# Attention probabilities turned by products with a diagonal of reciprocal denominators, in place of plain turns and a later division

## The chip, the cores and the metric

The kernel runs on one core of one Trainium2 chip. The metric is the device time of one execution in microseconds (us), as a median of several runs. Beside it one execution was recorded by the hardware profiler; its trace supplies every duration below. The engines are TensorE (PE for its products, PEld for the loads of their stationary side), VectorE (DVE), ScalarE (ACT), GpSimd (POOL) and SyncE (SP, which here only issues transfers). All data of the part in question is float32.

## The reference, cut to what matters

Two layers work on 1024 latent tokens and 256 context tokens. Inside a layer, one group of heads does windowed attention: a block of 128 queries sees its own block, the two neighbours and all 256 context keys, with one extra logit for each head (the sink) that takes part in the denominator only.

```
s_loc = jnp.einsum('bnikgd,bnjkd->bnkgij', qb, kw).astype(jnp.float32) * scale
s_ctx = jnp.einsum('bnikgd,bckd->bnkgic', qb, kc).astype(jnp.float32) * scale
...
probs = jax.nn.softmax(jnp.concatenate([s_loc, s_ctx, sink_l], axis=-1), axis=-1)
o = (jnp.einsum('bnkgij,bnjkd->bnikgd', probs[..., :n_loc].astype(v.dtype), vw)
     + jnp.einsum('bnkgic,bckd->bnikgd', probs[..., n_loc:n_loc + n_ctx].astype(vc.dtype), vc))
```

The result goes, with three other groups of heads, through an output projection, a residual with two layer norms, and a router for the experts that come next. In the first layer the context tokens go through the same steps, but read only context.

## The kernel before

`attend` does this part, once for each layer. It walks over tiles of 128 tokens: N = 10 tiles in the first layer (eight latent, two context), N = 8 in the second. Each engine has its own program, written out in order by a loop over `t` from 0 to N + 1, and the engines meet only at semaphores. The loop is staggered: in pass `t` the attention of tile `t`, the output projection and first norm of tile `t - 1`, and the second norm and router of tile `t - 2` are under way. There is no scheduler: an instruction that waits holds up everything behind it on its engine.

Four heads are handled as two pairs, 0 and 1. For a pair, TensorE computes scores, VectorE masks them and takes maxima (`maxima`), and ScalarE takes exponentials (`exps`), which also leave row sums in `sums`; the exponential of the sink is in `se`. `expd` counts the pairs for which this is done. TensorE then turns the unnormalised probabilities (`turn_probs`, 10 blocks of 128x128 in a latent tile, 4 in a context tile) through the two PSUM buffers `T`, four, four and two blocks at a time; ScalarE copies each group to `pT` (`copy_turned`) and counts `T_read`, and TensorE may not reuse a buffer of `T` before. `values` multiplies by V and leaves the head outputs in `O[:, 0:2]`.

Normalisation comes last. Once for each tile, VectorE adds up the four denominators and takes reciprocals (`denominators`), GpSimd multiplies the identity with them (`diagonals`, into `dg`, 128x512), TensorE spreads them over partitions with four products against ones (`spread_den`, into `O[:, 2:4]`), ScalarE copies these to `rb`, and VectorE multiplies `O[:, 0:2]` by `rb` (`heads`), which counts `o_ready`.

On VectorE the second norm of tile `t - 2` (`norm2`, which ends in a `tensor_scalar` at L214) stands after `maxima(t, 0)`. Its end, `norm2_done`, starts `modulate_rows` on GpSimd: two operations over 128x1024, L1137 and L1139, each with both inputs in SBUF. In the last two tiles of a layer VectorE does these itself. GpSimd's `add_one(0)` (L1131) waits for a transfer and stands at the head of GpSimd's program, ahead of the diagonals of tile 0.

Of the kernel before, what the change touches and what calls it, by code (L numbers as in the profile page):

```python
# [10 lines left out]
ALU = mybir.AluOpType  # L11
# [3 lines left out]
P = 128  # L15
# [7 lines left out]
HD = 64  # L23
# [127 lines left out]
def across(ap, n):  # L151

    return ap.unsqueeze(1).to_broadcast([ap.shape[0], n] + list(ap.shape[1:]))
# [880 lines left out]
def attend(nc, g, m, l):  # L1034
# [7 lines left out]
    with ExitStack() as ctx:  # L1042
# [12 lines left out]
        mx, mx2, den = sb("max_near", [P, 2]), sb("max_far", [P, 2]), sb("denominator", [P, NH])  # L1055
        dg, rb = sb("den_diag", [P, NH, P]), sb("den_rows", [P, 2, P])
        ys = [sb(f"mixT{i}", [P, 4, P]) for i in range(2)]
# [9 lines left out]
            sem(n) for n in ("sink_in", "small_in", "g1_in", "vec_in", "w_in", "ln1_in", "router_in"))  # L1067
        far_scored, scored, maxed, expd, den_ready, diag_ready = (
            sem(n) for n in ("far_scored", "scored", "maxed", "expd", "den_ready", "diag_ready"))
        T_full, T_read = [sem(f"turn_full{i}") for i in range(2)], [sem(f"turn_read{i}") for i in range(2)]  # L1070
        gate_full, sgu_done, rb_full, rb_read, pv_done, o_ready = (
            sem(n) for n in ("gate_full", "sgu_done", "rb_full", "rb_read", "pv_done", "o_ready"))
        y0_full, y1_full, y_used = (sem(n) for n in ("y0_full", "y1_full", "y_used"))
# [22 lines left out]
        with nc.Block() as block:  # L1096
# [31 lines left out]
            def _(pool):  # L1128
# [14 lines left out]

                def diagonals(t):
                    pool.wait_ge(den_ready, t + 1)
                    if t:
                        pool.wait_ge(rb_full, t)
                    nc.gpsimd.tensor_tensor(dg[:, :, :], across(g.k[:, K_ID:K_ID + P], NH), over(den[:, :], P), ALU.mult).then_inc(diag_ready, 1)

                def gain_rows(u):  # L1150
# [9 lines left out]
                for t in range(N + 2):  # L1160
                    if rtr(t):
                        norm_power(nc, pool, g, n2, t - 2)
                        if t - 2 < N - 2:
                            modulate_rows(t - 2)
                    if att(t):
                        diagonals(t)
                    if t == N - 1 and N > LT:
                        add_one(1)
                    if prj(t):
                        if t == 1:  # L1170
                            pool.wait_ge(ln1_in, 32)
                        norm_power(nc, pool, g, n1, t - 1)
                        if t - 1 < N - 1:
                            gain_rows(t - 1)

            @block.vector
            def _(v):
# [34 lines left out]

                def denominators(t):
                    v.wait_ge(expd, t * 2 + 2)
                    if t:
                        v.wait_ge(diag_ready, t)
                    small(nc.vector.tensor_tensor(den[:, :], sums[:, 1, :], se[:, :], ALU.add))
                    done()
                    small(nc.vector.tensor_tensor(den[:, :], den[:, :], sums[:, 0, :], ALU.add))
                    done()  # L1220
                    nc.vector.reciprocal(den[:, :], den[:, :]).then_inc(den_ready, 1)

                def heads(t):
                    v.wait_ge(rb_read, t + 1)
                    nc.vector.tensor_tensor(ys[t % 2][:, 0:2, :], O[:, 0:2, :], rb[:, :, :], ALU.mult).then_inc(o_ready, 1)

# [58 lines left out]
                for t in range(N + 2):  # L1285
                    if att(t):
                        maxima(t, 0)
                    if rtr(t):
                        norm2(t - 2)
                    if prj(t):  # L1290
                        residual(t - 1, 0)
                    if att(t):
                        maxima(t, 1)
                        if t == 0:
                            v.wait_ge(small_in, 80)
                        gate_out(t)
                        denominators(t)
                    if prj(t):
                        residual(t - 1, 1)
                        norm1(t - 1)  # L1300
                    if t == N - 1:
                        heads(t)
                    if rtr(t) and t != N:
                        h2_turned(t - 2)
                    if t < N - 1:
                        heads(t)

            @block.scalar
            def _(act):
                def exps(t, pair):  # L1310
                    act.wait_ge(maxed, t * 4 + pair * 2 + 2)
                    if t:
                        b, n = turn_of["probs", t - 1, pair, len(blocks(t - 1)) - 1]
                        act.wait_ge(T_full[b], n + 1)
                        if pair == 0:
                            act.wait_ge(den_ready, t)
# [26 lines left out]
                for t in range(N + 2):  # L1343
                    if t >= 3:
                        logits(t - 3)
                    if att(t):
# [3 lines left out]
                        act.wait_ge(pv_done, t * 2 + 2)  # L1350
                        nc.scalar.activation(rb[:, :, :], O[:, 2:4, :], ACT.Copy).then_inc(rb_read, 1)
                    if t >= N:
# [14 lines left out]
            def _(pe):  # L1367
# [30 lines left out]
                def turn_probs(t, pair):  # L1398
                    pe.wait_ge(expd, t * 2 + pair + 1)
                    flat = pr[pair][:, :, :].rearrange("p a n -> p (a n)")  # L1400
                    for j, group in enumerate(blocks(t)):
                        turn(("probs", t, pair, j), [flat[:, b * P:(b + 1) * P] for b in group])

# [14 lines left out]
                def gate(t):  # L1418
# [4 lines left out]
                    mm.then_inc(gate_full, 1)  # L1423

                def spread_den(t):
                    pe.wait_ge(diag_ready, t + 1)
                    for pair in range(2):
                        for kv in range(NKV):
                            mm = nc.tensor.matmul(O[kv * HD:(kv + 1) * HD, 2 + pair, :], g.k[:, K_ONE:K_ONE + HD], dg[:, 2 * kv + pair, :], start=True, stop=True)
                    mm.then_inc(rb_full, 1)  # L1430

# [39 lines left out]
                for t in range(N + 2):  # L1471
# [24 lines left out]
                    if att(t):  # L1496
                        spread_den(t)
                        values(t, 1)
# [757 lines left out]
```

## Time and profile before

| what | value |
|---|---|
| median of 3 runs | 2593.94 us (2593.25 to 2599.5) |
| the profiled execution | 2593.13 us, span 2591.3 us |
| TensorE busy over the span | 2337.7 us (90%) |
| VectorE, ScalarE, GpSimd busy | 939.7, 406.8, 464.0 us |
| `attend`, first layer | some 351.8 to 640 us from the span's start |
| `attend`, second layer | some 1600 to 1842 us |
| L1395, turns of probabilities | 336 rows, 54.6 us busy |
| L1148, diagonals on GpSimd | 18 operations of 1.04 us |

Outside `attend` nothing is touched by the change: most of the span lies in the experts (L2046 and the lines behind it). A reader takes from the table that the execution that was profiled is as long as the others, and that TensorE is the engine with least slack over the whole; whether it is so in `attend` is read from the trace of that stretch.

### The profile page before, as it was taken

How to read it: one execution, taken by the hardware profiler on the slowest of the kernel's cores; microseconds unless marked ns; L12 is line 12 of the kernel's file. 1: busy time of each engine (PE TensorE's matmuls, PEld its weight loads, DVE VectorE, ACT ScalarE, POOL GpSimd, SP SyncE). 2: the span in 40 equal slices, each digit the busy share in tenths (PEclk: the TensorE clock that was granted, in tenths of full speed). 3: DMA queues.
4: the chain of work that ended last, by engine and by line, in shares of the span. 5: the costliest groups of instructions: out<-in, count | busy, mean ns of one | idle time of the engine just before them, and what ended most of it. 6: DMA issues, size and time to landing. Idle time of an engine off the chain costs nothing. (4 is left out here: it accounts for less than half of the span.)

```text
span 2591.3 us, 39013 instructions
## 1 busy us (share of the span) xinstructions
PE 2337.7 (90%) x15084; PEld 1629.2 (63%) x15084; DVE 939.7 (36%) x2319; ACT 406.8 (16%) x1057; POOL 464.0 (18%) x608
## 2 busy tenths in 40 slices
PE   7999879997499999999949997999389999999996
PEld 5999745654466666666639984555266666666652
DVE  1777746665401110110126565565611111111114
ACT  1011133321011111111111113233000000000000
POOL 0000103444011111111111111344111111111111
PEclk9999989998699999999979998999689999999998
DMA  9655430001679999999832103000289999999955
GB/s 357 202 172 157 147 114 17 17 26 49 235 299 393 387 395 388 387 392 401 344 138 96 49 19 146 29 25 17 106 345 398 384 382 391 391 386 394 377 230 213
DMA packets 130991, 608.69 MB, mean 235 GB/s; under 512 B 20840, under 2 KB 23912, under 8 KB 112208
## 3 DMA queue, kind: packets, MB, share of 16 engines
q1 hardware_dynamic: 113456, 569.60, 56.9%
q0 software_dynamic: 16864, 37.78, 3.8%
q8 instruction: 63, 1.03, 0.2%
q14 instruction: 32, 0.26, 0.0%
q10 hardware_dynamic: 576, 0.02, 0.0%
HBM read 599.39 MB, written 42.02 MB: 248 GB/s over the span
## 5 line engine op out<-in xcount | busy, mean ns | idle before, releaser
L2046 PEld LDWEIGHTS gate_up<-room,w_gate_up 128*128 128x128 f32 x4608 | 521.1, 193 | 31.6 <-issue 31.6
L2046 PE MATMUL gate_up<-room,w_gate_up 128*128 128x128 f32 x4608 | 528.0, 277 | 3.2 <-DVE room L1926 3.2
L2055 PE MATMUL down<-w_down,room 128*128 128x512 f32 x576 | 256.8, 599 | 0.0
L2063 PE MATMUL gate_up_short<-w_gate_up,room 128*64 128x512 f32 x1152 | 255.1, 595 | 0.0
L1935 DVE TENSOR_TENSOR room<-room,gate_up 128x128 f32<-128x128 f32 x144 | 41.4, 288 | 539.0 <-ACT room L1966 539.0
L2063 PEld LDWEIGHTS gate_up_short<-w_gate_up,room 128*64 128x64 f32 x1152 | 79.5, 137 | 171.3 <-issue 171.3
L2055 PEld LDWEIGHTS down<-w_down,room 128*128 128x128 f32 x576 | 106.5, 190 | 123.0 <-issue 120.5
L1657 POOL COPY rows_idx<-slot_token 128x1 int32 (+1 forms) x78 | 14.3, 183 | 777.7 <-PE rows_turned L2033 721.1
L1943 DVE TENSOR_TENSOR room<-room,gate_up_short 128x256 f32<-128x256 f32 x36 | 15.2, 421 | 369.1 <-ACT room L1973 369.1
L2076 PE MATMUL down<-w_down,room 128*64 128x512 f32 x576 | 131.5, 598 | 11.9 <-ACT room L1975 11.9
L1443 PE MATMUL proj<-w_out,mixT 128*128 128x512 f32 x288 | 129.5, 592 | 0.0
L1966 ACT ACTIVATE room<-gate_up 128x128 f32<-128x128 f32 x144 | 39.9, 277 | 552.6 <-PE gate_up L2046 552.6
L2033 PE MATMUL rows_turned<-consts,rows 128*128 128x128 f32 (+1 forms) x592 | 90.7, 286 | 27.2 <-DMA rows<-h_rows,rows_idx 27.2
L2033 PEld LDWEIGHTS rows_turned<-consts,rows 128*128 128x128 f32 (+1 forms) x592 | 75.1, 196 | 61.0 <-issue 56.6
L1926 DVE COPY room<-rows_turned 128x512 f32<-128x512 f32 (+1 forms) x148 | 76.1, 556 | 70.6 <-PE rows_turned L2033 70.6
L1443 PEld LDWEIGHTS proj<-w_out,mixT 128*128 128x128 f32 x288 | 54.7, 190 | 68.9 <-issue 68.9
L397 DVE SCALAR_TENSOR_TENSOR ada_sum<-ada_w,cond_silu,ada_sum 128x512 f32<-128x512 f32 x140 | 96.2, 745 | 4.8 <-DMA ada_w<-in_w_ada 1.6
L1660 POOL DMA_INDIRECT rows<-h_rows,rows_idx x78 | 78.7, 1010 | 66.5 <-POOL rows_idx L1657 48.7
L2076 PEld LDWEIGHTS down<-w_down,room 128*64 128x64 f32 x576 | 39.4, 136 | 79.2 <-issue 79.2
L1671 POOL DMA_INDIRECT expert_rows<-room,y_idx x36 | 36.7, 1019 | 225.0 <-DVE room L1941 113.4
L1395 PE MATMUL turn<-consts,probs 128*128 128x128 f32 x336 | 54.6, 299 | 22.0 <-ACT sink_exp L1323 12.7
L538 PE MATMUL bankC<-hT,w_in 128*128 128x128 f32 x640 | 74.1, 277 | 0.0
(365 smaller groups left out, 3206.2 us busy)
## 6 DMA issues: line engine op xcount, KB each, us to landing
w_gate_up<-in_w_exp_gate SPq DMA_DIRECT2D x72, 2048.0 KB, 8.5
w_down<-in_w_exp_down SPq DMA_DIRECT2D x72, 2048.0 KB
w_gate_up<-in_w_exp_up SPq DMA_DIRECT2D x72, 2048.0 KB, 13.3
ada_w<-in_w_ada SPq DMA_DIRECT2D x96, 512.0 KB, 4.8
h_rows<-h SPq DMA_DIRECT2D x18, 512.0 KB, 2.6
w_out<-in_w_out SPq DMA_DIRECT2D x2, 4096.0 KB, 13.4
w_in<-in_w_in SPq DMA_DIRECT2D x2, 3072.0 KB, 20.6
xn<-expert_rows SPq DMA_DIRECT2D x10, 512.0 KB, 4.1
```

The source lines that it names most:

```text
L397: op = nc.vector.scalar_tensor_tensor(acc[:, i, :], w_k, by, acc[:, i, :], ALU.mult, ALU.add)
L538: i = nc.tensor.matmul(out, lhsT(k), rhs(k), start=k == 0, stop=k == KT - 1)
L1395: tr = nc.tensor.transpose(T[b][:, i, :], src, ident)
L1443: mm = nc.tensor.matmul(Y[:, half, :], rows, wo[:, k, half * 512:(half + 1) * 512], start=j == 0, stop=j == KT - 1)
L1660: pool.indirect_dma_start(xg[q][rows, :], None, g.h2[:, :], bass.IndirectOffsetOnAxis(ap=idx[q][rows, 0:1], axis=0), bounds_check=NT * P - ...
L1926: c = nc.vector.tensor_copy(xT[q][:, 4 * h:4 * h + 4, :], T[:, 4 * h:4 * h + 4, 0:P if q == 0 else HP])
L1935: nc.vector.tensor_tensor(hid[:, j, :], silu[:, j % 2, :], H[j % 2][:, 1, :], ALU.mult).then_inc(hid_done, 1)
L2033: tr = nc.tensor.transpose(T[:, k, 0:rows], xg[q][0:rows, k::KT], g.k[0:rows, K_ID:K_ID + rows])
L2046: mm = nc.tensor.matmul(H[j % 2][:, o, :], wgu[0][:, o, k, j * P:(j + 1) * P], xT[0][:, k, :], start=k == 0, stop=k == KT - 1)
L2055: mm = nc.tensor.matmul(Y[:, h, :], hid[:, j, :], wd[0][:, j, h * 512:(h + 1) * 512], start=j == 0, stop=j == JT - 1)
L2063: mm = nc.tensor.matmul(Hs[c * HP:(c + 1) * HP, :, :], xT[1][:, k, :], wgu[1][:, :, k, c * 2 * P:(c + 1) * 2 * P], start=k == 0, stop=k == ...
L2076: mm = nc.tensor.matmul(Y[h * HP:(h + 1) * HP, 0, :], hidT_s[:, j % 2, j // 2 * HP:(j // 2 + 1) * HP], wd[1][:, j, h * 512:(h + 1) * 512], ...
```

## The change

Each block of probabilities is now turned by an ordinary product with a 128x128 diagonal of the reciprocals as moving side, so that what reaches `pT` is already normalised. For this the denominators have to be there before the turn. `denominators` runs for each pair, on VectorE, and makes the diagonals there too (128x256 for a pair); `turn_probs` waits for `diag_ready` of its pair where it waited for `expd`. `diagonals` on GpSimd, `spread_den` on TensorE, the copy to `rb` and `heads` are gone; ScalarE copies `O[:, 0:2]` to the mixer's input `ys`.

```
-                def diagonals(t):
-                    pool.wait_ge(den_ready, t + 1)
...
-                    nc.gpsimd.tensor_tensor(dg[:, :, :], across(g.k[:, K_ID:K_ID + P], NH), over(den[:, :], P), ALU.mult).then_inc(diag_ready, 1)
...
-                def denominators(t):
...
+                def denominators(t, pair):
+                    mine = lambda x: x[:, pair:NH:2]
+                    v.wait_ge(expd, t * 2 + pair + 1)
+                    small(nc.vector.tensor_tensor(mine(den), mine(sums[:, 1, :]), mine(se), ALU.add))
                     done()
+                    small(nc.vector.tensor_tensor(mine(den), mine(den), mine(sums[:, 0, :]), ALU.add))
                     done()
+                    small(nc.vector.reciprocal(mine(den), mine(den)))
+                    done()
+                    nc.vector.tensor_tensor(dg[:, pair, :, :], across(g.k[:, K_ID:K_ID + P], 2), over(mine(den), P), ALU.mult).then_inc(diag_ready, 1)
...
-                def heads(t):
-                    v.wait_ge(rb_read, t + 1)
-                    nc.vector.tensor_tensor(ys[t % 2][:, 0:2, :], O[:, 0:2, :], rb[:, :, :], ALU.mult).then_inc(o_ready, 1)
...
                     if rtr(t):
                         norm2(t - 2)
+                    if att(t):
+                        denominators(t, 0)
                     if prj(t):
                         residual(t - 1, 0)
...
                         gate_out(t)
-                        denominators(t)
+                        denominators(t, 1)
...
-                        nc.scalar.activation(rb[:, :, :], O[:, 2:4, :], ACT.Copy).then_inc(rb_read, 1)
+                        nc.scalar.activation(ys[t % 2][:, 0:2, :], O[:, 0:2, :], ACT.Copy).then_inc(o_ready, 1)
...
                 def turn_probs(t, pair):
-                    pe.wait_ge(expd, t * 2 + pair + 1)
+                    pe.wait_ge(diag_ready, t * 2 + pair + 1)
...
-                        turn(("probs", t, pair, j), [flat[:, b * P:(b + 1) * P] for b in group])
+                        b, n = turn_of["probs", t, pair, j]
+                        if n:
+                            pe.wait_ge(T_read[b], n)
+                        for i, k in enumerate(group):
+                            mm = nc.tensor.matmul(T[b][:, i, :], flat[:, k * P:(k + 1) * P], dg[:, pair, k // 5, :], start=True, stop=True)
+                        mm.then_inc(T_full[b], 1)
...
-                def spread_den(t):
-                    pe.wait_ge(diag_ready, t + 1)
-                    for pair in range(2):
-                        for kv in range(NKV):
-                            mm = nc.tensor.matmul(O[kv * HD:(kv + 1) * HD, 2 + pair, :], g.k[:, K_ONE:K_ONE + HD], dg[:, 2 * kv + pair, :], start=True, stop=True)
-                    mm.then_inc(rb_full, 1)
```

VectorE, in the first layer, from the end of the second norm of tile `t - 2` to the residual of tile `t - 1`, before:

```order
L206 MEMSET norm_spare 128x1
L207 BN_AGGR norm_mv<-norm_stats 128x2
L214 TENSOR_SCALAR h_0_0<-x_res,norm_mv,norm_rstd 128x1024
L1237 TENSOR_TENSOR h_1_0<-proj,mod_0 128x512
L1239 SCALAR_TENSOR_TENSOR x_res<-x_res,h_1_0 128x512
```

The same place now:

```order
L214 TENSOR_SCALAR h_0_0<-x_res,norm_mv,norm_rstd 128x1024
L1208 TENSOR_TENSOR denominator<-sums,sink_exp 128x2
L1210 TENSOR_TENSOR denominator<-denominator,sums 128x2
L1212 RECIPROCAL denominator<-denominator 128x2
L1214 TENSOR_TENSOR den_diag<-consts,denominator 128x256
L1226 TENSOR_TENSOR h_1_0<-proj,mod_0 128x512
L1228 SCALAR_TENSOR_TENSOR x_res<-x_res,h_1_0 128x512
```

Four operations now stand directly behind the `tensor_scalar` whose end starts GpSimd on L1137.

TensorE, from the values of pair 0 to the router in the same pass, before:

```order
L1414 MATMUL head_out<-probsT_0,v_tok 64x128 x10
L1395 MATMUL turn_0<-consts,probs_0 128x128 x10
L1395 MATMUL turn_0<-consts,h_0_0 128x128 x8
L1429 MATMUL head_out<-den_diag,consts 64x128 x4
L1414 MATMUL head_out<-probsT_0,v_tok 64x128 x10
L1463 MATMUL turn_0<-h2T,w_router 36x128 x8
```

The same place now:

```order
L1404 MATMUL head_out<-probsT_0,v_tok 64x128 x10
L1391 MATMUL turn_0<-den_diag,probs_0 128x128 x10
L1380 MATMUL turn_0<-consts,h_1_0 128x128 x8
L1404 MATMUL head_out<-probsT_0,v_tok 64x128 x10
L1446 MATMUL turn_0<-h2T,w_router 36x128 x8
```

The four spreading products are gone, and the turn of the probabilities has the diagonal as an input instead of the constants.

## Rows read from the trace of the kernel before

**Rows 1.** Busy times in one pass of the first layer's `attend`.

```profile
core 0: us, PE busy (x) PEld busy (x) DVE busy (x) ACT busy (x) POOL busy (x), PEclk, DMA share, GB/s
510.67:537.25 26.58, 25.82 (x161) 15.79 (x159) 16.41 (x42) 8.53 (x28) 12.29 (x10) 1.00 0.05 21
```

**Rows 2.** Timeline, one pass around pair 0's turn: start, length, engine, instruction.

```profile
464.32 0.21 ACT L1323 ACTIVATE sink_exp<-sink_diff 128x2 f32<-128x2 f32 x1
464.65 0.81 DVE L214 TENSOR_SCALAR h<-x_res,norm_mv,norm_rstd 128x1024 f32<-128x1024 f32 x1 [0.93 <-POOL norm_rstd L197]
465.54 2.37 POOL L1137 TENSOR_TENSOR h<-h,mod 128x1024 f32<-128x1024 f32 x1 [0.93 <-DVE h L214]
466.34 1.04 PE L1395 MATMUL turn<-consts,probs 128*128 128x128 f32 x8
467.37 1.09 DVE L1239 SCALAR_TENSOR_TENSOR x_res<-x_res,h 128x512 f32<-128x512 f32 x1
467.69 0.44 PE L1395 MATMUL turn<-consts,probs 128*128 128x128 f32 x2 [0.31 <-ACT probsT L1336]
467.98 2.68 POOL L1139 TENSOR_TENSOR h<-h,mod 128x1024 f32<-128x1024 f32 x1
468.05 0.59 PE L1378 MATMUL scores<-kT,qT 64*128 64x384 f32 x1
```

**Rows 3.** Instructions by tile (probs, head_out): count, nanoseconds least/median/most, first and last start.

```profile
L1395 PE MATMUL turn<-consts,probs x336: 272/273/477, 359.9 to 1809.1; 128*128 128x128 f32 x168
L1429 PE MATMUL head_out<-den_diag,consts x144: 272/273/473, 376.9 to 1810.9; 128*64 128x128 f32 x144
```

**Rows 4.** The page's groups: 128x128 products that run back to back.

```profile
L2046 PE MATMUL gate_up<-room,w_gate_up 128*128 128x128 f32 x4608 | 528.0, 277 | 3.2 <-DVE room L1926 3.2
```

**Rows 5.** Timeline, TensorE from pair 1's turn to its values, in the same pass layout.

```profile
451.99 1.09 PE L1395 MATMUL turn<-consts,probs 128*128 128x128 f32 x8
453.98 1.07 PE L1395 MATMUL turn<-consts,h 128*128 128x128 f32 x8
454.97 0.66 PE L1429 MATMUL head_out<-den_diag,consts 128*64 128x128 f32 x8
455.46 1.26 PE L1414 MATMUL head_out<-probsT,v_tok 128*64 128x128 f32 x20
```

**Rows 6.** Timeline, tile 0: the small additions of the denominators.

```profile
369.76 0.16 DVE L1217 TENSOR_TENSOR denominator<-sums,sink_exp 128x4 f32<-128x4 f32 x1 [1.51 <-ACT sink_exp L1323]
369.96 0.16 DVE L1219 TENSOR_TENSOR denominator<-denominator,sums 128x4 f32<-128x4 f32 x1
```

**Rows 7.** Timeline, pass 8: a small VectorE operation during a long one of GpSimd.

```profile
563.81 2.35 POOL L1155 TENSOR_TENSOR x_res<-x_res,ln 128x1024 f32<-128x1024 f32 x1
565.69 0.49 DVE L1197 TENSOR_TENSOR max_far<-max_near,max_far 128x2 f32<-128x2 f32 x1
```

**Rows 8.** Timeline, pass 10: VectorE and GpSimd starting almost together.

```profile
617.46 1.31 DVE L1270 SCALAR_TENSOR_TENSOR h<-x_res,norm_mv,mod 128x1024 f32<-128x1024 f32 x1
617.50 0.19 POOL L195 TENSOR_TENSOR norm_rstd<-norm_mv,consts 128x1 f32<-128x1 f32 x1 [1.65 <-DVE norm_mv L207]
```

**Rows 9.** Timeline, the two context tiles: GpSimd's second operation, TensorE's turn.

```profile
571.99 0.60 PE L1395 MATMUL turn<-consts,probs 128*128 128x128 f32 x4
572.34 2.35 POOL L1139 TENSOR_TENSOR h<-h,mod 128x1024 f32<-128x1024 f32 x1
...
596.43 2.36 POOL L1139 TENSOR_TENSOR h<-h,mod 128x1024 f32<-128x1024 f32 x1
...
597.50 0.60 PE L1395 MATMUL turn<-consts,probs 128*128 128x128 f32 x4
```

**Rows 10.** Timeline, tile 0: GpSimd's first long operation, and TensorE behind the diagonal.

```profile
372.93 2.78 POOL L1131 TENSOR_SCALAR mod<-mod 128x1024 f32<-128x1024 f32 x1 [20.66 <-DMA mod<-mods]
376.88 1.12 PE L1429 MATMUL head_out<-den_diag,consts 128*64 128x128 f32 x8 [3.65 <-POOL den_diag L1148]
```

**Rows 11.** Busy times, the stretch right behind that wait.

```profile
376.81:380.21 3.40, 3.33 (x30) 3.00 (x30) 0.00 (x0) 0.03 (x1) 0.02 (x1) 0.50 0.00 0
```

More of the change, by code:

```diff
@@ L1055, in attend @@
         mx, mx2, den = sb("max_near", [P, 2]), sb("max_far", [P, 2]), sb("denominator", [P, NH])
-        dg, rb = sb("den_diag", [P, NH, P]), sb("den_rows", [P, 2, P])
+        dg = sb("den_diag", [P, 2, 2, P])
         ys = [sb(f"mixT{i}", [P, 4, P]) for i in range(2)]
@@ L1067, in attend @@
             sem(n) for n in ("sink_in", "small_in", "g1_in", "vec_in", "w_in", "ln1_in", "router_in"))
-        far_scored, scored, maxed, expd, den_ready, diag_ready = (
-            sem(n) for n in ("far_scored", "scored", "maxed", "expd", "den_ready", "diag_ready"))
+        far_scored, scored, maxed, expd, diag_ready = (
+            sem(n) for n in ("far_scored", "scored", "maxed", "expd", "diag_ready"))
         T_full, T_read = [sem(f"turn_full{i}") for i in range(2)], [sem(f"turn_read{i}") for i in range(2)]
-        gate_full, sgu_done, rb_full, rb_read, pv_done, o_ready = (
-            sem(n) for n in ("gate_full", "sgu_done", "rb_full", "rb_read", "pv_done", "o_ready"))
+        gate_full, sgu_done, pv_done, o_ready = (
+            sem(n) for n in ("gate_full", "sgu_done", "pv_done", "o_ready"))
         y0_full, y1_full, y_used = (sem(n) for n in ("y0_full", "y1_full", "y_used"))
@@ L1142, in modulate_rows @@
                         nc.gpsimd.engine_nop().then_inc(vec_free, 1)
-                def diagonals(t):
-                    pool.wait_ge(den_ready, t + 1)
-                    if t:
-                        pool.wait_ge(rb_full, t)
-                    nc.gpsimd.tensor_tensor(dg[:, :, :], across(g.k[:, K_ID:K_ID + P], NH), over(den[:, :], P), ALU.mult).then_inc(diag_ready, 1)
                 def gain_rows(u):
@@ L1164, in _ @@
                             modulate_rows(t - 2)
-                    if att(t):
-                        diagonals(t)
                     if t == N - 1 and N > LT:
@@ L1211, in gate_out @@
                     nc.vector.tensor_tensor(out, out, m.u[:, :, at_tile(t)], ALU.mult).then_inc(sgu_done, 1)
-                def denominators(t):
[L1214 to L1217, printed above, removed]
+                def denominators(t, pair):
+                    mine = lambda x: x[:, pair:NH:2]
+                    v.wait_ge(expd, t * 2 + pair + 1)
+                    small(nc.vector.tensor_tensor(mine(den), mine(sums[:, 1, :]), mine(se), ALU.add))
                     done()
-                    small(nc.vector.tensor_tensor(den[:, :], den[:, :], sums[:, 0, :], ALU.add))
+                    small(nc.vector.tensor_tensor(mine(den), mine(den), mine(sums[:, 0, :]), ALU.add))
                     done()
-                    nc.vector.reciprocal(den[:, :], den[:, :]).then_inc(den_ready, 1)
-                def heads(t):
-                    v.wait_ge(rb_read, t + 1)
-                    nc.vector.tensor_tensor(ys[t % 2][:, 0:2, :], O[:, 0:2, :], rb[:, :, :], ALU.mult).then_inc(o_ready, 1)
+                    small(nc.vector.reciprocal(mine(den), mine(den)))
+                    done()
+                    nc.vector.tensor_tensor(dg[:, pair, :, :], across(g.k[:, K_ID:K_ID + P], 2), over(mine(den), P), ALU.mult).then_inc(diag_ready, 1)
                 def residual(u, half):
@@ L1300, in _ @@
                         norm1(t - 1)
-                    if t == N - 1:
-                        heads(t)
                     if rtr(t) and t != N:
                         h2_turned(t - 2)
-                    if t < N - 1:
-                        heads(t)
             @block.scalar
@@ L1314, in exps @@
                         act.wait_ge(T_full[b], n + 1)
-                        if pair == 0:
-                            act.wait_ge(den_ready, t)
                     for i in range(2):
@@ L1496, in _ @@
                     if att(t):
-                        spread_den(t)
                         values(t, 1)
```

## The prediction

> **What bounds the kernel now.** I first read the busy times of one pass of `attend` [rows 1]: in a pass of 26.58 us TensorE is busy for 25.82, at the full granted clock; VectorE for 16.4, GpSimd for 12.3, ScalarE for 8.5. So in a steady pass each microsecond that TensorE works more or waits longer is a microsecond of the run. Then I read the timeline of one pass (tile 4 of the first layer) around the place where the turn of pair 0 stands [rows 2]. TensorE reaches this turn at 466.34. The exponentials that it waits for ended at 464.53, so there is a slack of 1.8 us today. Within it VectorE is held until 465.46 by the `tensor_scalar` of the second norm, whose end starts GpSimd's L1137 at 465.54; L1139 follows at 467.98. The same timeline shows L1239 at 1.09 us; its least time is 0.69. It started at 467.37, inside L1137, and ended at 468.46, which is 0.55 us after L1137's end (467.91). L1139 in turn took 2.68 us instead of 2.36 [rows 2, 9]. Both engines read two tensors of SBUF there. A smaller case says it more sharply [rows 7]: an addition over two columns, started at 565.69 inside L1155, took 0.49 us and ended at 566.18, when L1155 ended (566.16); alone it would have been an addition like those of 0.16 us [rows 6]. I read this as: a VectorE operation with two SBUF inputs stands still until the GpSimd operation that runs is over, whatever its own size.
>
> **The change part by part.**
>
> *The turn on TensorE.* The count of instructions matters more than their length. Today 336 blocks are turned by 336 matmul rows, one for each block; the 72 spreading products, which are ordinary float32 products, have 144 rows, two for each [rows 3]. So the turn becomes 20 rows for a pair of a latent tile instead of 10. Rows of 128 columns that run back to back with full weights come at 528.0 us / 4608 = 0.115 us [rows 4], so 20 rows take 2.3 us, and about 0.1 us of handover to the next kind. Today pair 0's block occupies TensorE from 466.34 to 468.05, 1.71 us, because it waits for ScalarE's copy before its last two turns [rows 2]; at the slower rate that copy is done in time, and the wait goes. So pair 0 costs 2.36 - 1.71 = +0.65 us. For pair 1 the stretch to the next turn is 1.99 us (451.99 to 453.98) [rows 5]; ScalarE's copies then end it at about 2.65, +0.65 too. The spreading products leave: from 454.97 to 455.46, 0.49 us [rows 5]. Net +0.8 us of TensorE for a latent tile, bounded by +0.7 and by +1.9 (if neither wait goes). There are 14 steady latent tiles (7 in each layer): +11.2 us.
>
> The Trainium skill, "TensorE: Matmul & The Clock Gate", section Terms, says that the transpose mode of a matmul is four times faster for FP32. The rows here show a factor of two in instructions, 336 for 336 blocks against 144 for 72 products [rows 3]. By the page the products would cost 20 rows more for each pair than I count.
>
> *Pair 0's denominators on VectorE.* They stand directly behind L214. The first addition follows L214 without a wait and ends at about 465.54, when GpSimd starts. The second needs the first and starts 0.20 us after it [rows 6], at about 465.57: 0.03 us after L1137. Who wins is decided by a pair of starts [rows 8]: L1270 on VectorE started at 617.46, 0.04 us before GpSimd's L195, and L195 still took its 0.19 us unhindered. So GpSimd goes first even with VectorE slightly ahead, and here VectorE is behind. The second addition then waits until L1137 ends, 467.91. The reciprocal (one tensor, about 0.2 us) lets L1139 start at 467.98. The diagonal (128x256, two SBUF inputs) meets L1139 and waits until it ends: 467.98 + 2.36, the undisturbed length [rows 9], = 470.34. Behind that end it needs between 0.02 us (the two columns of rows 7) and 0.55 (the 512 of L1239); by size 0.28. TensorE starts some 0.08 us later, at 470.70. Against 466.34 this is a stall of 4.4 us. Behind it in VectorE's queue stands the residual of tile `t - 1`, first half, and then `maxima(t, 1)`; both have their inputs later than the diagonal or shortly behind, since the scores of pair 1 also move by 5 us. Behind the waiting turn on TensorE stands everything else of the pass. So nothing hides it.
>
> This holds for passes in which GpSimd modulates and TensorE turns a latent tile: tiles 2 to 7 in both layers, 12 x 4.36 = 52.3 us. In tile 1 GpSimd has no such work and the slack of 1.8 us covers four operations of about 1 us. In the context tiles L1139 ends at 574.70 and 598.79 and the turns stand at 571.99 and 597.50 [rows 9]: with the same 0.36 behind, stalls of 3.1 and 1.7 us, and 4 rows more, 0.45 us, for pair 0 (for pair 1 these rows and the missing spread cancel): 5.6 us.
>
> *Pair 1's denominators.* They come after `gate_out`, when GpSimd has finished its modulation, and are ready some 2 us before TensorE reaches this turn behind the second half of the projection. Cost nothing; without that cover about 1 us a tile.
>
> *Tile 0.* Today TensorE waits 3.65 us for the diagonal behind L1131 [rows 10]. Pair 1's additions meet L1131 and wait for its end, 375.71; the diagonal is ready at about 376.8, when the spread starts today. Behind it now stands a turn of 2.4 us (twice that at half clock) instead of a spread of 0.5 to 0.9. +2 to +3.5 us, I take 2.5, in two layers 5 us. If L1131 with its one tensor did not hold VectorE, this would be near nothing.
>
> *The clock.* Behind the wait of 3.65 us the granted clock was 0.50 of full, that is 1.2 GHz instead of 2.4, for 3.4 us in which TensorE was busy for 3.33 [rows 10, 11]. Half of that is lost, 1.7 us. The stalls of 4.4 us are longer than that wait, so I give each of the 14 stalls 1.7 us: 23.8 us. The ends are 0 and 3.4 us each.
>
> *What leaves elsewhere.* GpSimd's 18 diagonals, ScalarE's copy (which stays, to another place) and VectorE's `heads` lie beside TensorE's work; they give nothing.
>
> **Sum.** 52.3 + 11.2 + 5.6 + 5 + 23.8 = 97.9 us, on the profiled execution's 2593.1 us: 2691. The median of the runs is 0.8 us above that execution, so I say 2692.
>
> **The rivals.**
>
> *Only the first of GpSimd's operations holds the diagonal.* If the second addition slips in ahead of L1137, the reciprocal follows, and the diagonal goes through in the gap at 467.91, as L1239 does today. The turn starts at 468.27, a stall of 1.9 us: 23.2 us for 12 tiles, 11.2 for the rows, 1.5 for context, 5 for tile 0, and the clock perhaps half the time, 10. Sum 51, 2644 us. For it: the starts are only 0.03 us apart. Against: GpSimd went first from behind [rows 8].
>
> *Nothing is held.* Then the diagonal is ready four operations after L214, 465.46 + 0.2 + 0.2 + 0.2 + 0.4 = 466.5, and the stall is 0.2 us. The sum is 2.6 + 11.2 + 0.9 + 5 = 20, 2613 us. Against it stand the held operations [rows 2, 7].
>
> *Faster: TensorE only loses work.* If a product with the diagonal cost one row as a turn does, the blocks would stay as they are, 18 spreads of 0.49 us go, and with TensorE as the sole bound the waits of tile 0 go too, 3.65 us twice: -16 us, 2577. It decides when a product costs under about 1.2 rows. The counts speak against it [rows 3].
>
> *Dearer products.* Four rows each instead of two add 2.3 us for each of the 28 steady blocks and 0.9 for four of context, 68 us on top of the main case: 2760. The page named above says four times; here the count of rows speaks against it.
>
> **How the numbers follow.** Main case 0.72, first rival 0.12, nothing held 0.07, faster 0.04, dearer 0.03, others 0.02. The likeliest case alone spans 2668 (clock never falls) to 2716 (two such spells behind each stall, less the tiles in which it finds little work). The range must leave out no more than 2 in 10: from 2638, which takes in the first rival, to 2716. 0.3% of this run is 8 us, about what a measurement of this kernel can tell from no change: faster by more than that 0.05, within it 0.03, slower 0.92.
>
> **What would show it.** In the profile after: 672 rows for the turned blocks instead of 336; a pass of 33 to 34 us instead of 26.6; the second addition of pair 0 with a duration of about 2.3 us and the diagonal of pair 0 with about 2.5, both ending with GpSimd's operations; TensorE idle about 4.4 us before the turn of pair 0, released by VectorE's diagonal; the granted clock at half behind many of these. Wrong: short additions and a diagonal of 0.4 us throughout (then nothing is held); a diagonal that ends at L1137's end (then the first rival); a clock that stays full over the stalls (then 2668); 336 rows (then faster).

## The result and the profile after

| | before | after |
|---|---|---|
| median of the runs on the same chip | 2593.94 us | 2696.1 us (2694.34 to 2700.42) |
| ratio, 95% interval | 1 | 1.0389 (1.0376 to 1.0402) |
| profiled execution | 2593.13 us | 2700.42 us, span 2698.6 us |
| first `attend`, first scores to last router products | 288.2 us | 347.3 us |
| second `attend`, the same | 241.9 us | 289.5 us |

The change costs 102 us by the medians; 98 was forecast. The two stretches of `attend` alone grew by 59.1 + 47.6 = 106.7 us, and the span by 107.3 (the profiled execution is the longest of the five), so all but 0.6 us of it lies inside `attend`. Of the seven executions of the kernel before that stand beside e1 to e4 one took 9757.84 us, which no trace explains; it is in none of the ratios.

The page of the kernel after: busy times, and its group for the turn of the probabilities.

```profile
PE 2400.8 (89%) x15276; PEld 1693.3 (63%) x15276; DVE 1007.2 (37%) x2391; ACT 410.1 (15%) x1057; POOL 441.3 (16%) x590
L1391 PE MATMUL turn<-den_diag,probs 128*128 128x128 f32 x672 | 116.5, 345 | 72.7 <-DVE den_diag L1214 72.7
```

There are 672 rows where there were 336 [rows 3], and TensorE stands idle for 72.7 us in front of them, in 18 waits, released each time by VectorE's diagonal. Of these, 50.0 us are the waits of tiles 2 to 7 in the two layers; 15.6 us stand before the first turn of a layer, where the kernel before waits too (6.38 and 6.35 us, for ScalarE's exponentials). The same stretch as in [rows 2], the timeline of a steady pass of the kernel after:

```profile
550.10 0.21 ACT L1308 ACTIVATE sink_exp<-sink_diff 128x2 f32<-128x2 f32 x1
550.43 0.81 DVE L214 TENSOR_SCALAR h<-x_res,norm_mv,norm_rstd 128x1024 f32<-128x1024 f32 x1 [0.94 <-POOL norm_rstd L197]
551.16 0.15 DVE L1208 TENSOR_TENSOR denominator<-sums,sink_exp 128x2 f32<-128x2 f32 x1
551.32 2.34 POOL L1137 TENSOR_TENSOR h<-h,mod 128x1024 f32<-128x1024 f32 x1 [0.93 <-DVE h L214]
551.35 2.33 DVE L1210 TENSOR_TENSOR denominator<-denominator,sums 128x2 f32<-128x2 f32 x1
553.71 0.17 DVE L1212 RECIPROCAL denominator<-denominator 128x2 f32<-128x2 f32 x1
553.74 2.34 POOL L1139 TENSOR_TENSOR h<-h,mod 128x1024 f32<-128x1024 f32 x1
553.91 2.45 DVE L1214 TENSOR_TENSOR den_diag<-consts,denominator 128x256 f32<-128x256 f32 x1
556.29 0.68 DVE L1226 TENSOR_TENSOR h<-proj,mod 128x512 f32<-128x512 f32 x1
556.42 4.63 PE L1391 MATMUL turn<-den_diag,probs 128*128 128x128 f32 x20 [4.13 <-DVE den_diag L1214]
```

Two additions of the same form stand here, 0.19 us apart. One takes 0.15 us; the other starts 0.03 us behind GpSimd's L1137 and takes 2.33, to the end of L1137. The diagonal then takes 2.45, to just behind the end of L1139. At the lengths that the four have in e1 below, the diagonal would be ready at about 552.2; TensorE goes on at 556.42.

The busy times of a pass, of the stretch behind the wait, and of pair 1's turn up to the turn of h (columns as in [rows 1]):

```profile
543.32:577.53 34.21, 29.86 (x174) 19.96 (x172) 21.01 (x45) 8.73 (x28) 10.88 (x9) 0.90 0.04 17
556.42:560.98 4.56, 4.56 (x21) 4.34 (x21) 1.92 (x4) 1.19 (x2) 0.00 (x0) 0.50 0.29 115
571.58:574.40 2.82, 2.61 (x22) 2.40 (x21) 1.80 (x6) 1.33 (x3) 0.74 (x2) 1.00 0.02 6
```

The pass takes 34.21 us where [rows 1] had 26.58. Right behind the wait the clock was granted at 0.50, that is 1.2 GHz, and the turn of pair 0, which takes 2.51 us at the full clock (e1 below), takes 4.63. The mean of the ten passes of tiles 2 to 6 in the two layers is 34.02, against 26.56 before.

Tile 0 of the first layer, and the last context tile, in the timeline of the kernel after:

```profile
373.02 2.78 POOL L1131 TENSOR_SCALAR mod<-mod 128x1024 f32<-128x1024 f32 x1 [20.86 <-DMA mod<-mods]
373.03 1.05 DVE L1208 TENSOR_TENSOR denominator<-sums,sink_exp 128x2 f32<-128x2 f32 x1 [1.51 <-ACT sink_exp L1308]
374.51 0.42 DVE L1214 TENSOR_TENSOR den_diag<-consts,denominator 128x256 f32<-128x256 f32 x1
374.99 4.64 PE L1391 MATMUL turn<-den_diag,probs 128*128 128x128 f32 x20 [0.92 <-DVE den_diag L1214]
...
619.48 2.45 DVE L1214 TENSOR_TENSOR den_diag<-consts,denominator 128x256 f32<-128x256 f32 x1
621.99 1.53 PE L1391 MATMUL turn<-den_diag,probs 128*128 128x128 f32 x8 [2.54 <-DVE den_diag L1214]
```

In tile 0 an addition started 0.01 us behind L1131 is held for 1.05 us only, though L1131 runs for 2.78: the prediction had it held to the end.

### The profile page after: what moved, and what is told of

Read it like the earlier page. It is cut to its first block and busy times, and to the rows that moved or that the text cites. A ratio compares the mean times of both kernels' runs of the same rounds, so it can differ in the third digit from the quotient of the medians.

```text
span 2698.6 us, 39417 instructions
## 1 busy us (share of the span) xinstructions
PE 2400.8 (89%) x15276; PEld 1693.3 (63%) x15276; DVE 1007.2 (37%) x2391; ACT 410.1 (15%) x1057; POOL 441.3 (16%) x590
## 5 line engine op out<-in xcount | busy, mean ns | idle before, releaser
L2028 PE MATMUL gate_up<-room,w_gate_up 128*128 128x128 f32 x4608 | 528.8, 277 | 3.2 <-DVE room L1908 3.2
L1391 PE MATMUL turn<-den_diag,probs 128*128 128x128 f32 x672 | 116.5, 345 | 72.7 <-DVE den_diag L1214 72.7
L1391 PEld LDWEIGHTS turn<-den_diag,probs 128*128 128x128 f32 x672 | 107.4, 249 | 89.9 <-DVE den_diag L1214 86.0
L1321 ACT ACTIVATE probsT<-turn 128x512 f32<-128x512 f32 (+1 forms) x100 | 52.4, 529 | 239.5 <-PE turn L1391 239.5
```

The costliest lines, as they stand in the source:

```text
L1321: nc.scalar.activation(dst, src, ACT.Copy).then_inc(T_read[b], 1)
L1391: mm = nc.tensor.matmul(T[b][:, i, :], flat[:, k * P:(k + 1) * P], dg[:, pair, k // 5, :], start=True, stop=True)
L2028: mm = nc.tensor.matmul(H[j % 2][:, o, :], wgu[0][:, o, k, j * P:(j + 1) * P], xT[0][:, k, :], start=k == 0, stop=k == KT - 1)
```

## The experiments

The theory under test is the prediction's: operations of VectorE with two tensors in SBUF stand still while a two-input operation of GpSimd runs, two of them one after the other; what this adds to a pass is the wait, the clock behind it, and twice the rows on TensorE. The rivals are that the products or the extra operations themselves are dear, and that another wait lies under the visible one. Experiments e1 to e4 were measured together, beside the kernel before at 2596.14 us (2594.87 without the longest of its seven); e5 to e8 later on the same chip, beside it at 2594.8; e9 on another chip, beside it at 2592.64. Each ratio is to the kernel before that stands beside it. The kernel after stands beside none of them; its 2696.1 us belong with 2593.94 of the kernel before, so a difference to it is good to some 2 us.

### e1: the same operations, ahead of the `tensor_scalar`

```
+                        rows_stats(nc, v, s, x, n2)
+                        denominators(u + 2, 0)
+                        v.wait_ge(n2.rstd_ready, u + 1)
+                        nc.vector.tensor_scalar(h, x, n2.mv[:, 0:1], n2.rstd[:, :], ALU.subtract, ALU.mult).then_inc(norm2_done, 1)
```

> The changed kernel with one thing moved: from tile 2 on, the four operations of pair 0's denominators stand in the second norm, between its aggregation and the tensor_scalar whose end starts GpSimd's modulation, so they run while GpSimd has nothing long to do. My theory (the stall of 4.1 us a pass is VectorE held by GpSimd's two long operations, because both read two tensors of SBUF): the additions take 0.16 us, the diagonal 0.42, TensorE's wait before pair 0's turn goes, the clock stays full in steady passes, and what is left of the slowdown is TensorE's rows: 14 tiles x 0.8 + 1 for context + some 4 for tile 0, 2610 us, 2605 to 2617. Rival 1 (the price is the products themselves, dearer than two rows): 2670 or more. Rival 2 (the second norm, now 1 us later, makes another wait, such as the modulation colliding with the residual): 2625 to 2650.

Measured: 2612.49 us, ratio 1.0057 (1.0039 to 1.0076). Its timeline and one pass:

```profile
525.72 0.16 DVE L1208 TENSOR_TENSOR denominator<-sums,sink_exp 128x2 f32<-128x2 f32 x1 [0.85 <-ACT sink_exp L1311]
525.92 0.16 DVE L1210 TENSOR_TENSOR denominator<-denominator,sums 128x2 f32<-128x2 f32 x1
526.31 0.42 DVE L1214 TENSOR_TENSOR den_diag<-consts,denominator 128x256 f32<-128x256 f32 x1
527.50 2.51 PE L1394 MATMUL turn<-den_diag,probs 128*128 128x128 f32 x20
...
518.47:546.18 27.71, 27.50 (x174) 17.99 (x172) 18.16 (x45) 8.69 (x28) 11.22 (x9) 1.00 0.05 21
```

The same four operations, put where GpSimd has nothing to do, take 0.16, 0.16, 0.17 and 0.42 us, and TensorE finds the diagonal ready. 84 us of the 102 go with the place of four instructions in one queue. A pass of 27.71 us, 27.50 of it busy, is what the change costs in TensorE's work alone: 1.14 us more than before.

### e2: the products alone, in the kernel before

```
-                        turn(("probs", t, pair, j), [flat[:, b * P:(b + 1) * P] for b in group])
+                            mm = nc.tensor.matmul(T[b][:, i, :], flat[:, k * P:(k + 1) * P], ident, start=True, stop=True)
```

> The kernel before with one thing changed: probabilities are turned by ordinary products with the identity instead of by the transpose mode; denominators, spreading and the division stay as they were. It prices the product by itself. My theory (two rows for each instead of one, and ScalarE's copies cover part of it): +0.65 us for each of 28 steady blocks, 18 us, some 4 us more in the two tiles 0, which run at half clock, and 1 to 2 in the context tiles: 2617 us, 2612 to 2624. Rival (the transpose mode is four times faster for float32): 20 rows more a block, 2680 or more. Rival (TensorE has room for it): 2594 to 2600.

Measured: 2615.42 us, ratio 1.0072 (1.0054 to 1.0090). A pass:

```profile
514.72:542.87 28.15, 27.94 (x180) 18.43 (x181) 16.49 (x41) 8.70 (x28) 12.28 (x10) 1.00 0.05 20
```

28.15 us is 1.58 over the pass of before with 20 rows more, and 0.44 over e1's: that is what the spreading products cost (0.49 was read from [rows 5]). Dearer products are out.

### e3 and e4: the hold, and the clock behind it

e3 cuts GpSimd's two operations over 1024 columns into four over 512, in the kernel after.

```
+                    nc.gpsimd.tensor_tensor(h[:, lo], h[:, lo], vec[:, 2, lo], ALU.mult).then_inc(halves, 1)
+                    nc.gpsimd.tensor_tensor(h[:, hi], h[:, hi], vec[:, 2, hi], ALU.mult).then_inc(scaled2, 1)
+                    pool.wait_ge(halves, 2 * u + 1)
+                    nc.gpsimd.tensor_tensor(h[:, lo], h[:, lo], vec[:, 1, lo], ALU.add).then_inc(halves, 1)
```

> The changed kernel with GpSimd's two modulating operations over 1024 columns cut into four over 512. My theory (a held VectorE operation stands still for the whole of the one GpSimd operation that runs, and goes in the gap behind it): the second addition is held for about 1.15 us instead of 2.33, the diagonal for about 1.2 instead of 2.45, TensorE waits about 1.8 us instead of 4.13 before pair 0's turn; 12 passes x 2.3 = 28 us less, and the clock falls less often (0 to 20 us more): 2650 to 2668. Rival (VectorE is held until GpSimd has no more work of this kind): 2690 or more, with the diagonal held for over 3 us.

Measured: 2644.86 us, ratio 1.0192 (1.0173 to 1.0210). Its timeline:

```profile
535.05 1.26 POOL L1139 TENSOR_TENSOR h<-h,mod 128x512 f32<-128x512 f32 x1 [0.93 <-DVE h L214]
535.08 1.26 DVE L1216 TENSOR_TENSOR denominator<-denominator,sums 128x2 f32<-128x2 f32 x1
536.57 1.25 DVE L1220 TENSOR_TENSOR den_diag<-consts,denominator 128x256 f32<-128x256 f32 x1
537.87 2.62 PE L1397 MATMUL turn<-den_diag,probs 128*128 128x128 f32 x20 [1.86 <-DVE den_diag L1220]
```

Half as long an operation of GpSimd holds VectorE half as long: 1.26 and 1.25 us for 2.33 and 2.45, and the wait is 1.86. Five of the ten waits of this length come with a stretch of half clock. The time lies below the range expected, which counted twelve passes only: in the context tiles the waits of 2.54 and 3.08 us fall to 0.26 and none. The hold has the length of GpSimd's operation, not of VectorE's.

e4 gives TensorE 32 turns of the identity to do in the wait, which nobody reads.

```
+                    if pair == 0 and t >= 2:
...
+                        for i in range(32):
+                            nc.tensor.transpose(T[b][:, i % 4, :], ident, ident)
                     pe.wait_ge(diag_ready, t * 2 + pair + 1)
```

> The changed kernel with 32 turns of the identity put on TensorE ahead of its wait for pair 0's diagonal, from tile 2 on; their results are overwritten. They fill 3.5 us of a stall of 4.4 us and change nothing else. My theory (the granted clock falls because TensorE idles for 4.1 us, and this costs about 1.7 us behind each of 14 stalls): the clock stays at full in the steady passes, passes take about 32 us instead of 33.6 to 34.3, and the run about 2672 us (2665 to 2680), although TensorE issues some 450 more rows. Rival (the half clock has another cause, such as the load on TensorE): 2696 or more with the same spells.

Measured: 2673.73 us, ratio 1.0298 (1.0279 to 1.0316): 22.4 us less than the kernel after, with 32 instructions more in each pass. Timeline and a pass:

```profile
511.46 3.66 PE L1389 MATMUL turn<-consts 128*128 128x128 f32 x32
515.81 2.62 PE L1397 MATMUL turn<-den_diag,probs 128*128 128x128 f32 x20 [0.69 <-DVE den_diag L1214]
...
534.55:566.71 32.16, 31.26 (x207) 21.47 (x204) 21.07 (x45) 8.69 (x28) 10.92 (x9) 1.00 0.05 18
```

The clock stays full and the turn of pair 0 is back at 2.62 us; the stall itself stays, since the filler only lies in it. e4 minus e1, 32.16 - 27.71 = 4.45 us, is the stall with no change of clock (0.11 of it is pair 0's turn, which takes 2.55 us to the next product behind a wait and 2.44 in e1); after minus e4, 34.02 - 32.16 = 1.86, is the clock.

### e5: the diagonal by operations with one tensor

```
+                    diag = lambda i: nc.vector.tensor_scalar(dg[:, pair, i, :], g.k[:, K_ID:K_ID + P], den[:, 2 * i + pair:2 * i + pair + 1], None, ALU.mult)
```

> The changed kernel with the diagonal made by two tensor_scalar operations over 128x128 (one SBUF tensor, the identity, and a reciprocal per partition) instead of one tensor_tensor over 128x256 with two SBUF tensors. The two additions in front stay as they are. Theory A (only the second tensor input goes through what GpSimd shares): the second addition is held by the first modulating operation as before, the diagonals are not held by the second, TensorE waits about 2.2 us instead of 4.13 before pair 0's turn, and the run takes 2645 to 2668 us. Theory B (a tensor_scalar of VectorE runs faster than one column a cycle, 1024 columns in 0.81 us in the second norm, and is held by GpSimd's operations as well): the first diagonal takes over 2 us, the wait is 4.4 us, 2695 to 2705. I give B 0.6.

Measured: 2695.47 us, ratio 1.0393 (1.0377 to 1.0409), nothing gained. Timeline:

```profile
519.10 2.34 POOL L1139 TENSOR_TENSOR h<-h,mod 128x1024 f32<-128x1024 f32 x1
519.27 2.57 DVE L1214 TENSOR_SCALAR den_diag<-consts,denominator 128x128 f32<-128x128 f32 x2
521.90 3.72 PE L1394 MATMUL turn<-den_diag,probs 128*128 128x128 f32 x20 [4.26 <-DVE den_diag L1214]
```

Where nothing runs on GpSimd the same pair takes 0.61 us. So the hold isn't a matter of two input tensors on VectorE's side alone; this `tensor_scalar` is held too. It is not so of every operation with one tensor: in e7 below a reciprocal starts inside L1138 and takes 0.17 us. The Trainium skill, "SBUF — State Buffer", section "Who interferes with whom", says that `tensor_scalar` can enter modes that use the port pair shared with GpSimd; e5 agrees.

### e7: one reduction in place of two additions

The exponential of the sink is written beside the sums, and one `tensor_reduce` adds the three.

```
-                    small(nc.vector.tensor_tensor(mine(den), mine(sums[:, 1, :]), mine(se), ALU.add))
-                    done()
-                    small(nc.vector.tensor_tensor(mine(den), mine(den), mine(sums[:, 0, :]), ALU.add))
+                    small(nc.vector.tensor_reduce(mine(den), sums[:, :, pair:NH:2].rearrange("p a h -> p h a"), AX, ALU.add))
```

> The changed kernel with the two additions of a pair's denominators replaced by one reduction over a tile that holds both sums and the sink's exponential, so one SBUF input instead of two. The diagonal stays a tensor_tensor with two. This is the first rival of the prediction made real. My theory: the reduction and the reciprocal are not held, the diagonal reaches its place inside GpSimd's first modulating operation, is held until that ends and goes in the gap ahead of the second; TensorE waits about 1.7 to 1.9 us instead of 4.13 before pair 0's turn, and the run takes 2640 to 2652 us, like the kernel with halved modulation. Rival (a small operation with one SBUF input is held too): 2690 or more.

Measured: 2634.94 us, ratio 1.0161 (1.0145 to 1.0176). Timeline and a pass:

```profile
502.00 0.15 DVE L1209 TENSOR_REDUCE denominator<-sums 128x2 f32<-128x6 f32 x1
502.16 2.34 POOL L1138 TENSOR_TENSOR h<-h,mod 128x1024 f32<-128x1024 f32 x1 [0.93 <-DVE h L214]
502.19 0.17 DVE L1211 RECIPROCAL denominator<-denominator 128x2 f32<-128x2 f32 x1
502.39 2.40 DVE L1213 TENSOR_TENSOR den_diag<-consts,denominator 128x256 f32<-128x256 f32 x1
504.84 2.62 PE L1390 MATMUL turn<-den_diag,probs 128*128 128x128 f32 x20 [1.71 <-DVE den_diag L1213]
...
523.64:553.33 29.69, 27.77 (x176) 17.91 (x170) 19.90 (x43) 8.70 (x28) 10.96 (x9) 1.00 0.05 19
```

Without the second addition only the diagonal is held, by the first of GpSimd's operations alone. This is the prediction's first rival, made real by taking out one instruction of 0.16 us: the wait falls from 4.13 to 1.71 us and 61 us go. The ten passes of tiles 2 to 6 take 29.87 us in the mean, and twelve at 34.02 - 29.87 us are 50 of them; the rest lies in tile 0 and in the context tiles of the first layer, where of the waits of 2.54 and 3.08 us only 0.67 of the second is left. The time lies below the range expected; the clock stayed full in the steady passes but one (tile 2 of the first layer, behind a wait of 1.94 us).

### e8: as e7, with the diagonals made by ScalarE

```
                     nc.scalar.activation(se[:, pair:NH:2], sd[:, pair:NH:2], ACT.Exp).then_inc(expd, 1)
+                    act.wait_ge(den_ready, t * 2 + pair + 1)
+                    for i in range(2):
+                        d = nc.scalar.activation(dg[:, pair, i, :], g.k[:, K_ID:K_ID + P], ACT.Copy, scale=den[:, 2 * i + pair:2 * i + pair + 1])
+                    d.then_inc(diag_ready, 1)
```

> As the kernel with one reduction, and the two diagonals of a pair are made by ScalarE (copies of the identity scaled by the reciprocal of the partition), directly behind its exponentials. Nothing that TensorE waits for is now an operation with two SBUF inputs on VectorE. My theory: no operation of this chain is held, the diagonal is ready 0.1 to 0.4 us after TensorE could start, no spells of half clock in steady passes; what is left is TensorE's rows: 2611 to 2621 us, like the kernel with pair 0's denominators moved ahead. Rival (ScalarE's two operations delay its copies of turned blocks or the exponentials of pair 1): 2625 to 2645.

Measured: 2613.84 us, ratio 1.0074 (1.0059 to 1.0090). Timeline and a pass:

```profile
527.48 0.69 ACT L1308 ACTIVATE den_diag<-consts,denominator 128x128 f32<-128x128 f32 x2 [1.23 <-DVE denominator L1211]
...
519.24:547.23 27.99, 27.77 (x173) 17.91 (x171) 16.12 (x41) 10.09 (x32) 11.22 (x9) 1.00 0.05 20
```

ScalarE makes the diagonals while GpSimd's first operation runs and is not held. With the denominators still behind the `tensor_scalar`, this comes to within 1.4 us of e1, by another way.

### e9: GpSimd's first operation with one input

L1137 is replaced by an operation with one tensor; the scale of the second norm is left out.

```
-                    nc.gpsimd.tensor_tensor(h[:, :], h[:, :], vec[:, 2, :], ALU.mult).then_inc(scaled2, 1)
+                    nc.gpsimd.tensor_scalar(h[:, :], h[:, :], 0.0, None, ALU.add).then_inc(scaled2, 1)
```

> The changed kernel with GpSimd's first modulating operation (h times the scale, two SBUF tensors) replaced by a tensor_scalar that adds 0 to h (one SBUF tensor); the scale of the second norm is so left out in all but the last two tiles of a layer. In the changed kernel's tile 0 an operation of this form on GpSimd, 2.78 us long, held a VectorE addition for only 1.05 us from its start, and the diagonal behind it ran free. Theory A (a one-input operation of GpSimd holds VectorE only for the first 1.05 us): pair 0's second addition takes about 1.05 us instead of 2.33, the diagonal 0.42 us instead of 2.45, TensorE waits about 0.8 us instead of 4.13, no spells of half clock in steady passes, 2620 to 2640 us. Theory B (the case in tile 0 was something else, and every long operation holds to its end): the second addition takes about 2.8 us, 2695 to 2705.

Measured: 2659.62 us, against 2592.64 of the kernel before, ratio 1.0259 (1.0229 to 1.0289). Timeline, and the page's group of the experts' first product:

```profile
529.44 2.78 POOL L1137 TENSOR_SCALAR h<-h 128x1024 f32<-128x1024 f32 x1 [0.94 <-DVE h L214]
529.45 1.03 DVE L1210 TENSOR_TENSOR denominator<-denominator,sums 128x2 f32<-128x2 f32 x1
530.72 0.42 DVE L1214 TENSOR_TENSOR den_diag<-consts,denominator 128x256 f32<-128x256 f32 x1
531.20 2.62 PE L1391 MATMUL turn<-den_diag,probs 128*128 128x128 f32 x20 [0.81 <-DVE den_diag L1214]
...
L2028 PE MATMUL gate_up<-room,w_gate_up 128*128 128x128 f32 x4736 | 542.6, 277 | 3.4 <-DVE room L1908 3.4
```

L1137 is longer than before (2.78 us for 2.34) and holds the addition for only 1.03; the reciprocal and the diagonal then run at their own length while it goes on, and the wait is 0.81 us. The time lies above the range expected, for a reason outside `attend`: the missing scale changes what the router chooses, and the experts have 4736 rows where all other kernels here have 4608. The five groups of the experts' products that grew with it add up to 34.1 us more of TensorE (528.8 to 542.6 in this one). Less that, 2625.5 us lies in the range. The passes of tiles 2 to 6, which the experts don't touch, take 28.82 us in the mean, against 34.02 in the kernel after. Whether the hold is short because the operation has one input or because it is a `tensor_scalar` is not separated here.

### e6: the kernel before, with GpSimd's first operation moved

From [rows 10] the prediction read that TensorE waits 3.65 us because L1131 stands ahead of the first diagonals. e6 puts it behind them, in the kernel before.

```
-                add_one(0)
                 for t in range(N + 2):
...
                     if att(t):
                         diagonals(t)
+                    if t == 0:
+                        add_one(0)
```

> The kernel before with GpSimd's add_one(0), which waits for a transfer, put behind the diagonals of tile 0 instead of ahead of them. TensorE then doesn't wait for the diagonal of tile 0: 3.65 us in the first layer and 2.96 in the second go, and some of the half clock behind these waits. My theory: about 7 us, and 0 to 3 us of clock: 2584 to 2588 us. Rival (the output weights or the gates arrive late and take the place of the wait): 2592 or more.

Measured: 2588.34 us, ratio 0.9974 (0.9964 to 0.9983), the upper end of the range expected. Timeline:

```profile
372.23 1.04 POOL L1148 TENSOR_TENSOR den_diag<-consts,denominator 128x512 f32<-128x512 f32 x1 [18.52 <-DVE denominator L1222]
374.08 2.78 POOL L1131 TENSOR_SCALAR mod<-mod 128x1024 f32<-128x1024 f32 x1 [0.81 <-DMA mod<-mods]
374.98 0.94 PE L1430 MATMUL head_out<-den_diag,consts 128*64 128x128 f32 x8
```

TensorE no longer waits in front of the spread. It is the one kernel of the study that is faster than the kernel before: 6.5 us by the medians, which is small beside 2590 but outside the interval.

## Why the prediction was right, point by point

Terms of the sum and what was measured:

| term | forecast | measured |
|---|---|---|
| stall in 12 steady tiles | 4.36 each, 52.3 | 4.45 each (e4 less e1), 53.4 |
| rows on TensorE, 14 tiles | 0.8 each, 11.2 | 1.14 each in twelve (e1 less before), 2.3 for tile 1: 16.0 |
| clock in these 12 | 1.7 each, 20.4 | 1.86 each (after less e4), 22.3 |
| context tiles, with their clock | 5.6 + 3.4 | 11.4, as the remainder of the two stretches |
| tile 0, two layers | 5 | 1.5 + 2.1 = 3.6 |
| sum | 97.9 | 106.7, by which the two stretches grew; the span grew by 107.3 |

The measured sum takes tile 7 to be as tiles 2 to 6, and its line on context is a remainder, not a measurement of its own.

*The stall.* In the steady passes every link came as forecast: GpSimd started 0.03 us ahead, the second addition took 2.33 us, the reciprocal let L1139 go first, the diagonal took 2.45. e3 shows that the length is GpSimd's, e1 that without GpSimd there is no stall, e7 that the second addition is what loses the first of the two holds. The choice between the main case and the first rival leaned on one pair of starts [rows 8] and held in all steady passes, but that pair doesn't carry it. In the trace of before L1270 takes 1.31 us at all four of its places, with L195 starting 0.04 us behind it each time, so the row shows neither engine held. What came true is the order of the starts that the prediction worked out, 465.54 against 465.57: in the kernel after VectorE's addition started 0.02 to 0.03 us behind L1137 each time, and the first to start went first. "GpSimd goes first even with VectorE slightly ahead" is tested by no run. With so small a distance it was in part luck that the main case came and not the first rival, which e7 puts 61 us below it.

*The rows on TensorE.* The count was right, 672. The size was too low: a pair's turn to the next kind of product takes 2.45 us for pair 0 and 2.82 for pair 1 (the third window above), where 2.36 and about 2.65 were forecast. The prediction's step for pair 1, "ScalarE's copies then end it at about 2.65, +0.65 too", fell short the most: it is +0.83. Pair 0's +0.74 for +0.65, and the spread at 0.44 (e2 less e1) for 0.49, are most of the rest.

*The clock.* The step "I give each of the 14 stalls 1.7 us" was near in the mean. In the trace of after each of the ten waits of tiles 2 to 6 comes with a stretch of half clock, of 3.4 us four times and of 6.8 us six times. The short ones begin 0.7 to 1.3 us behind the start of the turn, the long ones 1.6 to 2.1 ahead of it, inside the wait; passes with the short one take about 33.6 us and with the long one 34.2 to 34.4. e4 shows it is worth 22 us of the total.

*Tile 0.* "Pair 1's additions meet L1131 and wait for its end" was wrong: the addition was held for 1.05 us of 2.78, the diagonal took 0.42, and the turn stood at 374.99, not behind 376.8. What was lost instead is in the turns at half clock (4.64 us each). In the sum this error is 1.4 us; e9 shows the same behaviour in twelve tiles, where it is worth some 62 (12 passes at 34.02 - 28.82 us).

*The context tiles.* Stalls of 3.1 and 1.7 us were forecast, 2.54 and 3.08 came. The step took the distance between GpSimd's operations and the turn from the kernel before, where TensorE reached the two turns 2.07 and 3.49 us behind the start of L1137; in the kernel after it reached them 2.56 and 2.02 us behind. The second was mis-sized by nearly half. Each comes with 6.8 us of half clock, where 1.7 us of loss were counted. Why the distances changed was not looked into.

*The rivals.* "Nothing is held" gave 2613; e1 and e8, in whose steady passes nothing of this chain is held, came at 2612.5 and 2613.8. "Faster" fell with the rows, and e2 prices it. The medians' 102 us against the profile's 107 is the spread of the runs, and it makes the forecast look nearer than its sum: by the medians it is 4 us off (2692 for 2696.1), by the profiled execution 9 (2691 for 2700.42), and four of the five terms were too low.

What stays open: why the stretch of half clock begins inside some waits and only behind others that are as long.

## What to carry to other kernels

Before small operations are put on VectorE's queue behind the instruction that starts GpSimd, look at what GpSimd then runs: four operations of 0.9 us together cost 4.4 us of the critical engine here, and nothing when put one instruction earlier (e1) or, in part, on ScalarE (e8). A chain of dependent small operations is held once for each GpSimd operation that it meets, so each link taken out may save a whole hold (e7: 61 us for one addition). And price a stall of TensorE with what the clock does behind it, two fifths of the wait again in this kernel (1.86 us on 4.45).

## What the runs showed of the hardware that was not expected

- The hold depends on GpSimd's operation. `tensor_tensor` over 128x1024 held VectorE for its whole 2.34 us; `tensor_scalar` with one tensor, of 2.78 us, held it for the first 1.03 to 1.05 us only (e9, and L1131 in tile 0 of the first layer of the kernel after; in the second layer a diagonal that started 0.37 us behind L1131 took 0.95 us for 0.42). The Trainium skill, "SBUF — State Buffer", section "Who interferes with whom", says, of VectorE's two-port modes, that the engine that issues first has the shared ports for its whole instruction and the other blocks fully; the first agrees with that and the second does not.
- VectorE's `tensor_scalar` over one 128x128 tensor is held as well (two in 2.57 us for 0.61, e5), a `reciprocal` over two columns isn't (0.17 us inside L1138, e7).
- Filling a wait with useless work made the kernel 22.4 us faster (e4). The ten waits of 1.71 and 1.72 us in e7 came with no fall of the clock (of the two in tile 2, one of 1.94 us did and one of 1.93 didn't), those of 1.86 in e3 with one in five of ten, those of 4.1 to 4.4 us in the kernel after with one each time.
